# Half steps of the output product in front of the fourth attention, earlier table loads, filter norms on channel columns, and a third slot for half modulation units

## The reference, cut to what matters

```
mod = silu(c) @ ada_w + ada_b                  # six modulation rows of 2048
h = rmsnorm(x) * (1 + sc1) + sh1
o_a, o_b, o_c, o_d = four attention mixers(h @ w_in)   # 8 heads of 64 each
#   o_d = gate0 * compressed(15 blocks) + gate1 * selected + gate2 * window
x = x + g1 * (concat(rmsnorm(o_m) for m) @ w_out)
x = x + g2 * mixture_of_16_experts(...)
# second block
h = sin-MLP(positions) @ w4 * decay            # filters, forward and backward
k = [h_fwd, 0, h_bwd[:0:-1]];  k = k / sum(|k|, over positions)
k_f = rfft(k);  y = long convolution with k_f, spatial gating, output product
x = x + swiglu(...)
```

## Time and profile before

| | |
|---|---|
| median of 3 runs | 2988.32 us (2987.99 to 2994.21) |
| profiled execution | 2990.0 us |
| its span, first to last instruction | 2987.8 us |
| mean granted TensorE clock | 0.953 |
| TensorE / VectorE / ScalarE busy | 91% / 63% / 43% |
| data moved | 651.10 MB |

### The profile page before, as it was taken

One profiled execution on the slowest core, in us unless ns is written; L12 is line 12 of the kernel. 1 busy time (PEld: TensorE's weight loads), 2 busy tenths in 40 slices (PEclk: granted clock), 3 DMA queues, 4 the chain that ended last, 5 costly groups with the idle time before them and its releaser, 6 DMA issues.

```text
span 2987.8 us, 36422 instructions
## 1 busy us (share of the span) xinstructions
PE 2721.8 (91%) x14284; PEld 2275.7 (76%) x14284; DVE 1880.4 (63%) x2425; ACT 1276.5 (43%) x1540; POOL 28.9 (1%) x50
## 2 busy tenths in 40 slices
PE   3769998897999999999698898999899999999997
PEld 1258887676788787777498396999778888888886
DVE  6987755576666888888766544454555544445444
ACT  2024543442444577777433043533344444443443
POOL 1000000000000000000000000000000000000000
PEclk9789998797999999999899997999999999999999
DMA  9787675351777899999354152554455555555553
GB/s 347 302 331 268 247 290 182 118 196 42 253 249 264 277 332 372 372 360 368 145 183 178 61 204 86 182 183 170 154 183 174 192 193 189 193 187 196 187 194 113
DMA packets 181342, 651.10 MB, mean 218 GB/s; under 512 B 12363, under 2 KB 12428, under 8 KB 136920
## 3 DMA queue, kind: packets, MB, share of 16 engines
q1 hardware_dynamic: 170208, 593.53, 55.9%
q0 software_dynamic: 8160, 37.17, 3.3%
q10 hardware_dynamic: 2840, 18.56, 1.7%
HBM read 641.82 MB, written 13.68 MB: 219 GB/s over the span
## 4 chain that ended last, share of the span: by engine, by line
PE 69%; DVE 14%; DMA 8%; ACT 5%; issue 3%; DVEq 0%; ACTq 0%; SPq 0%
PE ps L1586 68%; DMA raw<-in_stream 6%; DVE w_lo L923 3%; DVE raw L1002 2%; ACT w_hi L588 2%; DMA under_r<-in_stream 1%; DVE under_r L1020 1%; ACT arena L703 1%; ACT arena L609 1%; DVE arena L984 1%; DVE arena L1082 0%; DVE ps L1136 0%; PE ps L1685 0%; DVE arena L1098 0%; DVE h_lo L974 0%
## 5 line engine op out<-in xcount | busy, mean ns | idle before, releaser
L923 DVE TENSOR_TENSOR w_lo<-raw,w_hi 128x1024 fp32r<-128x1024 f32 x968 | 1170.2, 1223 | 800.4 <-ACT w_hi L588 797.4
L588 ACT ACTIVATE w_hi<-raw 128x1024 fp32r<-128x1024 f32 x968 | 1010.8, 1057 | 940.4 <-PE ps L1586 845.8
L1586 PE MATMUL ps<-w_hi,h_hi 128*128 128x512 f32 x1216 | 476.8, 392 | 15.9 <-DVE h_lo L1545 10.0
L1586 PE MATMUL ps<-w_hi,r_hi 128*128 128x512 f32 x1184 | 469.6, 397 | 14.2 <-DVE w_lo L923 7.1
L1586 PE MATMUL ps<-w_lo,h_hi 128*128 128x512 f32 x1216 | 475.1, 391 | 0.0
L1586 PE MATMUL ps<-w_hi,h_lo 128*128 128x512 f32 x1216 | 475.1, 391 | 0.0
L1586 PE MATMUL ps<-w_lo,r_hi 128*128 128x512 f32 x1184 | 462.6, 391 | 0.0
L1586 PE MATMUL ps<-w_hi,r_lo 128*128 128x512 f32 x1184 | 462.5, 391 | 0.0
L1586 PE MATMUL ps<-h_hi,w_hi 128*128 128x256 f32 x1536 | 443.6, 289 | 17.0 <-DVE w_lo L923 8.5
L1586 PE MATMUL ps<-h_lo,w_hi 128*128 128x256 f32 x1536 | 440.1, 287 | 0.0
L1586 PE MATMUL ps<-h_hi,w_lo 128*128 128x256 f32 x1536 | 439.8, 286 | 0.0
(11 more groups left out here) (268 smaller groups left out, 1839.9 us busy)
## 6 DMA issues: line engine op xcount, KB each, us to landing
raw<-in_stream SPq DMA_DIRECT2D x524, 1024.0 KB, 5.5
under_r<-in_stream SPq DMA_DIRECT2D x80, 512.0 KB, 5.3
arena<-in_mod_units ACTq DMA_DIRECT2D x16, 1024.0 KB, 4.9
bias_skew<-bias_rows POOLq DMA_DIRECT2D x4, 1536.0 KB, 21.4
filters<-arena POOLq DMA_DIRECT2D x4, 1280.0 KB, 5.1
arena<-filters POOLq DMA_DIRECT2D x4, 1280.0 KB, 6.0
x<-in_x POOLq DMA_DIRECT2D x1, 2048.0 KB, 19.7
arena<-bias_skew POOLq DMA_DIRECT2D x2, 1024.0 KB, 7.5
```

What stands on the lines that cost most here:

```text
L588: act.activation(dst, src, ACT.Copy).then_inc(hi_ready, 1)
L923: dve.tensor_tensor(low, src, high, ALU.subtract).then_inc(lo_ready, 1)
L1586: return pe.matmul(o, a, b, start=start, stop=stop)
```

## The change

1. *Filter norms on channel columns.* TensorE multiplies the absolute taps (as weights) with one column of ones, which gives the sums as 128x4; VectorE takes the reciprocal of that. ScalarE makes four diagonal matrices of it, TensorE spreads them with the matrix of ones, and ScalarE copies the result to `rnorm`. The row's `memset` goes: its taps come from a copy of the hidden layer whose first column is zero.
2. *A third slot.* Half units aside have three places, and each is loaded when the third last is summed up. The third place lies in part where the filters were, so SyncE waits for the last filter store.
3. *Table loads.* `spread_rows(1)`, three of the four compression loads and `spread_rows(3)` are issued during and after the first attention and in the second.
4. *The gap.* Half steps 0 to 7 of the output product, the splits of half steps 3 to 10, six half units aside and the first `part_out` stand between the parts of the compression. The fourth attention has one half step a turn and half units in ten turns. The compression's scores and transposes use banks 2 and 3.
5. `nsa_out` multiplies both gates in one instruction.

```diff
-FOURTH_HALVES = 16
+FOURTH_HALVES, GAP_HALVES, GAP_ASIDES = 16, 8, 6
...
+        rn_cols, rn_diag = stat[:, 156:160], at(13856, 4, P)
...
-            half = slice(j % 2 * HALF, (j % 2 + 1) * HALF)
+            half, last = slice(j % 2 * HALF, (j % 2 + 1) * HALF), under_r[:, 1, D + HALF:2 * D]
             if j < ASIDE_HALVES - FOURTH_HALVES:
-                return under_r[:, 1, D + j % 2 * HALF:D + (j % 2 + 1) * HALF], c_row[:, half]
-            return under_r[:, j % 2, D + HALF:2 * D], c_fourth[:, half]
+                return (under_r[:, 1, D:D + HALF], last, at(11936, HALF))[j % 3], c_row[:, half]
+            return (under_h[:, 0, 0:HALF], last, under_h[:, 0, HALF:D])[j % 3], c_fourth[:, half]
...
-            return range(3 * t // 2, 3 * (t + 1) // 2) if t < 16 else range(0)
+            return range(GAP_HALVES + t, GAP_HALVES + t + 1) if t < 16 else range(0)
...
-                if j >= 2:
-                    sp.wait_ge(sem("aside_done"), j - 1)
+                if j >= 3:
+                    sp.wait_ge(sem("aside_done"), j - 2)
                 if j == ASIDE_HALVES - FOURTH_HALVES:
-                    sp.wait_ge(sem("c_moved"), 1)
+                    sp.wait_ge(half_done, 8 * gp)
...
             weight(4)
+            sp.wait_ge(sem("kf_stored1"), 32)
+            aside(2)
...
+            for k in range(5):
+                part_weight(k)
+            aside(used + 3)
+            aside(used + 4)
+            aside(used + 5)
+            part_weight(6)
+            aside(used + 6)
+            aside(used + 7)
+            aside(used + 8)
+            used += GAP_ASIDES
...
+            pool.wait_ge(sem("att_out"), 2)
+            spread_rows(1)
+            pool.wait_ge(sem("att_out"), 16)
+            load("ld_cmp", (w1v, d["w1v"]), (w2c, d["w2kv"]), (peT, d["pe"]))
+            pool.wait_ge(sem("att_out"), 18)
+            spread_rows(3)
             pool.wait_ge(sem("att_out"), 16 * 2)
-            spread_rows(1)
             toeplitz(1, toep2)
-            load("ld_cmp", (w1k, d["w1k"]), (w1v, d["w1v"]), (w2c, d["w2kv"]), (peT, d["pe"]))
-            spread_rows(3)
+            load("ld_cmp", (w1k, d["w1k"]))
...
+            act.wait_ge(sem("sin_out"), 3)
+            act.activation(at(F_R, 1, parts=64), at(F_H, 1, parts=64), ACT.Copy, scale=0.0).then_inc(sem("sin_out"), 1)
+            act.activation(at(F_R + 1, P - 1, parts=64), at(F_H + 1, P - 1, parts=64), ACT.Copy).then_inc(sem("sin_out"), 1)
...
+                act.wait_ge(sem("rn_ready"), b + 1)
+                for q in range(4):
+                    ins = act.activation(rn_diag[:, q, :], ident, ACT.Copy, scale=rn_cols[:, q:q + 1])
+                ins.then_inc(sem("rn_act"), 1)
+                if b >= 2:
+                    act.wait_ge(sem("spectrum_out"), 5 * (b - 1))
+                act.wait_ge(sem("rn_spread"), b + 1)
+                copy(rnorm[b % 2], ps[:, 2, :]).then_inc(sem("rn_act"), 1)
...
             exps(16, 8, True, "d_q", qT2)
+            hi(gp, 3)
             norm_root("mixB", ("att_out", 48), 512, mix, mix_junk)
+            hi(gp, 4)
...
+            hi(gp, 5)
             act.wait_ge(sem("c_moved"), 1)
             norm_hi("mixB", r_hi, 4, mixf, 8)
+            hi(gp, 6)
+            hi(gp, 7)
             for r in range(4):
...
+                if r == 1:
+                    part_out(0)
+                if r < 3:
+                    hi(gp, 8 + r)
...
-                    if n == 1:
-                        ch(ins)
-                        ins = dve.memset(taps[b % 2][0:1, 1, :], 0.0)
...
-                ch(dve.reciprocal(rnorm[b % 2], ps[:, 2, :]))
+                if b:
+                    dve.wait_ge(sem("rn_act"), 2 * b)
+                dve.reciprocal(rn_cols, ps[:, 2, 0:4]).then_inc(sem("rn_ready"), 1)
...
             scores(16, 8, True, head_out, toep2, "d_q")
+            lo(gp, 3)
             mixer_unit("mixB", 48)
+            lo(gp, 4)
...
-            mixer_split(1, "mixB", 2)
+            lo(gp, 5)
             dve.wait_ge(sem("cmp_exp"), 1)
             dve.tensor_tensor(v15(cp), v15(cp), keep, ALU.mult).then_inc(sem("cmp_p"), 1)
+            mixer_split(1, "mixB", 2)
+            lo(gp, 6)
...
+            lo(gp, 7)
+            first_fourth = ASIDE_HALVES - FOURTH_HALVES
+            aside_half(first_fourth)
+            aside_half(first_fourth + 1)
+            lo(gp, 8)
+            aside_half(first_fourth + 2)
+            lo(gp, 9)
...
+                if q == 0:
+                    aside_half(first_fourth + 3)
+                    lo(gp, 10)
+                    aside_half(first_fourth + 4)
+                    aside_half(first_fourth + 5)
...
-                for half in range(TH):
-                    ch(dve.tensor_tensor(rden[:, half:half + 1], rden[:, half:half + 1],
-                                         gates[:, half, 3 * h + branch:3 * h + branch + 1], ALU.mult))
+                ch(dve.tensor_tensor(rden, rden, gates[:, :, 3 * h + branch], ALU.mult))
...
+                pe.wait_ge(sem("abs_ready"), 4 * b + 4)
+                if b:
+                    pe.wait_ge(sem("rn_act"), 2 * b)
+                for q in range(4):
+                    for n in range(4):
+                        ins = mm(ps[:, 2, q:q + 1], taps_abs[b % 2][:, n, q * P:(q + 1) * P], ones[:, 0:1], n == 0, n == 3)
                 ins.then_inc(sem("norm_mm"), 1)
+
+            def norm_spread(b):
+
+                pe.wait_ge(sem("rn_act"), 2 * b + 1)
+                for q in range(4):
+                    ins = mm(ps[:, 2, q * P:(q + 1) * P], ones[:, :], rn_diag[:, q, :])
+                ins.then_inc(sem("rn_spread"), 1)
...
             ins.then_inc(sem("cmp_s"), 1)
+            part(0)
+            part(1)
             turn("mixB", 4, mix)
+            part(2)
+            part(3)
             pe.wait_ge(sem("cmp_p"), 1)
             for r in range(4):
...
                 ins.then_inc(sem("cmp_t"), 1)
+                part(4 + r)
                 pe.wait_ge(sem("cmp_pt"), r + 1)
...
-            pe.wait_ge(sem("att_out"), 50)
```

More of the change, by code:

```diff
@@ L464, in _, with part_weight @@
                 for _ in range(ASIDE[k]):
-                    aside(used + 2)
+                    aside(used + 3)
                     used += 1
+            def part_weight(k):
+                if k % 2 == 0 and len(ASIDE) // 2 + k // 2 + 5 < BASE["moe"]:
+                    weight(len(ASIDE) // 2 + k // 2 + 5)
+            for k in range(5):
+                part_weight(k)
+            aside(used + 3)
+            aside(used + 4)
[5 more added lines that the diff above has]
+            used += GAP_ASIDES
             for t in range(16):
                 for k in share(t):
[L469 to L472, removed]
+                    part_weight(k)
+                if t < FOURTH_HALVES - GAP_ASIDES:
+                    aside(used + 3)
                     used += 1
@@ L682, in values_out, with part_out @@
                 return step
+            def part_out(cb):
+                act.wait_ge(half_done, 8 * gp + 6 * cb + 6)
+                copy(abc_sum[:, :, 512 * cb:512 * cb + 512], ps[:, 6:8, :]).then_inc(sem("part_out"), 1)
             def exps(first, n, sink, beside=None, dst=None, partial=False):
@@ L689, in exps @@
                 for t in range(n + 1):
-                    if partial and t and t % 4 == 0:
-                        cb = t // 4 - 1
-                        act.wait_ge(half_done, 8 * gp + 6 * cb + 6)
-                        copy(abc_sum[:, :, 512 * cb:512 * cb + 512], ps[:, 6:8, :]).then_inc(sem("part_out"), 1)
+                    if partial and t % 6 == 4:
+                        part_out(t // 6 + 1)
                     if t < n:
@@ L1651, in make_taps @@
                         pe.wait_ge(sem("taps_ready"), 4 * b + n - 1)
-                    mm(ps[:, n % 2, :], arena[0:64, F_H + (n // 2) * P:F_H + (n // 2 + 1) * P],
+                    rows_of = F_R if n == 1 else F_H + (n // 2) * P
+                    if 4 * b + n == 1:
+                        pe.wait_ge(sem("sin_out"), 5)
+                    mm(ps[:, n % 2, :], arena[0:64, rows_of:rows_of + P],
                        w4[:, b, (n % 2) * 512:(n % 2 + 1) * 512]).then_inc(sem("taps_mm"), 1)
             def taps_norm(b):
-                for n in range(4):
-                    pe.wait_ge(sem("abs_ready"), 4 * b + n + 1)
-                    ins = mm(ps[:, 2, :], ones[:, :], taps_abs[b % 2][:, n, :], n == 0, n == 3)
-                ins.then_inc(sem("norm_mm"), 1)
+                pe.wait_ge(sem("abs_ready"), 4 * b + 4)
[4 more added lines that the diff above has]
+                        ins = mm(ps[:, 2, q:q + 1], taps_abs[b % 2][:, n, q * P:(q + 1) * P], ones[:, 0:1], n == 0, n == 3)
+                ins.then_inc(sem("norm_mm"), 1)
+            def norm_spread(b):
[3 more added lines that the diff above has]
+                ins.then_inc(sem("rn_spread"), 1)
             make_taps(0)
@@ L1724, in attend @@
```

(18 more changed lines are left out.)

24 lines of the change are left out of this document (14 added, 10 removed).

## The result

The changed kernel takes 2969.8 us (median of four runs, 2965.1 to 2973.9) against 2989.7 for the kernel before (four runs, 2988.0 to 2994.2; the table ahead of the prediction has three of them): a ratio of 0.9926, 95% interval 0.9913 to 0.9939. Measured once more beside its variants it gives 2973.4 against 2989.8, ratio 0.9939 (0.9927 to 0.9951). So it is faster by 0.6 to 0.7%, 16 to 20 us. The forecast was 2967 with a range of 2955 to 2982. The profiled execution took 2971.0 (span 2968.9), 19 less than the one of before; its sum was forecast at 2968.2.

The account below looks back on a forecast made before the run. VectorE was taken to bound the prologue, and a VectorE-ScalarE chain the fourth attention, despite TensorE's 91%. Gains 13.3 + 6.4 + 2.1 = 21.8 us off 2990.0 give 2968.2; with the median 1.7 lower, forecast 2967, range 2955 to 2982.

Parts of the forecast that it names:

- What bounds: Whole kernel: TensorE works 91% of the span, but VectorE sets the pace in the first 180 us.
- the transfers set the pace: Rival, chance 0.18: the stream fails at 332 GB/s or half units land as late as now; 2977 us.
- Norms: Prologue: smaller reciprocals and no memsets on VectorE save 13.3 us, bounds 5 and 16.
- The reciprocal wait: Prologue sign: VectorE's wait for the norm sum near 5 us in the first block, none later.
- Third slot and tables: 404 to 485 us: TensorE's waits for half units and following half clock go; 6.4 us gained, bounds 0 and 9.
- The two waits of TensorE: 404 to 485 us: TensorE's waits for low parts, 4.4 us, taken as gone.
- The gap: Before the fourth attention: work moved in makes its first scores reach VectorE 12.3 us later.
- a gap at half clock: Rival, chance 0.13: the stretch before the fourth attention stays at half clock, costing 15.6 us; 2983 us.
- the filling does not fill: Rival, chance 0.05: half steps queue serially at half clock before the fourth attention, adding 41 us there; 2995 us.
- The fourth attention: Fourth attention: one half step a turn, not bound by TensorE; 15 us less, with 0.6 of tail taken off.
- the ring: Fourth attention: VectorE's scores, ScalarE's exponentials, copy and split, VectorE's low part set the turn; 5.73 us with one half step.
- The multiply: Attention outputs: one fewer multiply each, hidden while VectorE waits for ScalarE; priced at nothing, 2.6 us without that cover.

Follow-up runs that it names:

- old_norms: Changed kernel with the filter norms taken back to the 128x512 reciprocal and the zero-row memset; 2984.8 us, ratio 0.9976 to the kernel before.
- norm_twice: Changed kernel with every column of the filter norms computed twice, 32 instead of 16 one-column products a block; 2986.6 us, ratio 0.9982 to the kernel before.
- slots_tables: Changed kernel with two places for half units and GpSimd's table loads in the old order; 2982.8 us, ratio 0.9968 to the kernel before.
- two_slots: Changed kernel with two places for half units instead of three, table loads in their new place; 2977.8 us, ratio 0.9946 to the kernel before.
- hi_first4: Changed kernel with ScalarE's copy for a later split at the head of the turn, fourth attention only; 2965.1 us, ratio 0.9911 to the kernel before.
- hi_all_gap_undone: Changed kernel with ScalarE's copy at the turn's head in all four attentions, and half steps, splits and half units back in the fourth; 2945.9 us, ratio 0.9843.
- gap_undone: Changed kernel with half steps, splits and half units back in the fourth attention, third slot kept; 2976.8 us, ratio 0.9949 to the kernel before.

## Why the prediction was right, point by point

**What bounds.** Right for the prologue: VectorE is busy 29.4 of 30 us with the same stream, and what is taken from it comes off the end (old_norms, norm_twice). The rival that the transfers set the pace has fallen: the stream kept up at 339 GB/s, above the 332 it was said to need, and no wait for it appeared inside the modulation runs.

**Norms, 13.3 forecast.** 11.0 us between the first splits, 11.5 counted from the chunk with the DMA wait, 10.7 in the experiment. The first block gave 1.2 and not 1.8: from that chunk (49.03 before) to the end of the division it took 18.4 us before and 17.2 after. The price of a column in the first block was right (6.98 us for 32 instructions, 0.218 each, the upper bound), and so was its reason, the slow pace of this stretch: in the second block the same 32 take 3.63 us, 0.113 each, below the lower bound of 0.13. But the columns start at 59.48 and not at 58.4; 0.44 of that is a later start of the stream, the other 0.6 is the first block's shortfall, and VectorE waits 0.47 in it for a tap product. The reciprocal wait was forecast "near 5" and is 3.12. That figure did not follow from the prediction's own sum, which has the columns end at 65.4 and VectorE ready at 62.3 (64.05 less its wait of 1.06 and the memset's 0.65), a wait of 3.1. The later blocks gave 3 x 3.85 less 1.27: VectorE now waits 0.54, 0.27 and 0.46 us for TensorE's tap products, which the memset and the long reciprocal used to cover. That cover is the part that the sum missed.

**Third slot and tables, 6.4 forecast.** The ledger shows 3.7 to the compression, and slots_tables 5.7 in the same stretch; both lie within the bounds of 0 and 9. The waits lay behind the second attention, and that part alone shows more: from its last score to the compression's first product it takes 71.4 us before, 65.9 in the changed kernel, 66.0 and 66.1 with one measure undone and 71.0 with both. That is 5.2 to 5.5 of the 6.4 (other runs with the same three slots and tables took 63.5 to 66.4 in this part, so its size is known to some 2 us). The rest of the ledger's gap is 2.7 us lost ahead of it, between the first and the second attention (52.65 before, 55.37 now), and the repeat of the same program does not lose them (52.65 again): scatter. The two waits of TensorE (4.4 us) are gone and the 5.14 us at the compression are there, as said. What was missed is where the slot pays: either measure alone clears this stretch, and the third slot's own worth is in the gap. The prediction added up its parts as if they were independent.

**The gap, 12.3 forecast.** 12.3 measured, and the steps hold: the wait in front of half step 4 is 1.79 (forecast 1.4), the clock is at its lower level until after the scores, 0.74 in the next 7.2 us (1.9 us lost, forecast 2.1), 1.00 to 542.2, and 0.91 in the last 19.7, which costs 1.8 us (forecast 1.5 "for clock lost after such a wait"). The rival of a gap at half clock has fallen, and so has the one in which the filling does not fill. It held only because six half units could land in time; with two slots this part takes 47.0 us (two_slots) and 45.2 (slots_tables), not 42.65.

**The fourth attention, 15 less 0.6 forecast.** 17.05 measured. The turns are the forecast ones: seven of 5.73, two of 6.23 with a modulation sum, a first one of 5.36, and six of 4.58, the last one behind the last score. By the prediction's own span, from the first score to the division behind the last turn, it is 101.65 before and 85.40 now (561.86 to 647.26): 16.25 less, where 85.7 + 1.0 was forecast. The 1.0 for TensorE's own turn at the end did not come in this execution; in the repeat the last turns take 4.7 to 4.8. The other 0.8 us came behind it, where the eight transposes for mixer D's norm took 1.97 us before and 1.09 now; the prediction had put 0.6 us on the wrong side there. That the ring and not TensorE sets these turns, its main claim, is shown by hi_first4 for the attention of now. For the one of before it holds by a narrow margin: its pair of turns took 12.6 us on VectorE where TensorE, busy for 98.54 of 98.60 us, made its scores 7.47 and 4.75 us apart, 12.2 a pair, and ran ahead. The same layout with the ring shortened takes 90.2 us from first to last score (hi_all_gap_undone) against 94.4 (gap_undone), so "not bound by TensorE" was worth 4.2 us there, against 11.35 in the attention of now.

**The multiply, 0 forecast.** 0 in the turns.

**The sum.** 11.0 + 3.7 + 4.8 = 19.5 against 21.8, with 0.6 lost behind. Three terms were each off by two to three us, and the errors partly cancel. One of the three is scatter (the 2.7 us behind the first attention); the cover of the norms and the attention's gain were mis-sized. So the forecast was right within 3 us with some luck: the mechanisms held, and their sizes did less well than the whole shows.

## What to carry to other kernels

An engine that looks busy in a stage may still be waiting inside a ring of others: compare the turn with the engine's own work in it (4.75 us for TensorE against turns of 5.73 here), then ask which member of the ring does work in it that nobody in this turn needs. Putting that work in front of the wait instead of behind it was worth 38 us, twice the whole change, for four lines moved. Where the engine has enough work of its own, as TensorE in the fourth attention of before, the same ring costs little. Parts of a change that supply and use the same buffers are not to be added: price the consumer with and without the supply, and each cure for a stall with the other one in place.

## What the runs showed of the hardware that was not expected

**The clock falls in different places in executions of one kernel.** Behind the first attention TensorE stands still for a while; windows of 6 us, first in the profiled execution of the changed kernel, then in its repeat, which is 1.7 us later in its work:

```profile
290.00:296.00 6.00, 3.80 (x27) 3.33 (x25) 4.20 (x12) 3.25 (x9) 0.00 (x0) 0.87 0.70 254
296.00:302.00 6.00, 6.00 (x32) 6.00 (x32) 3.08 (x13) 3.00 (x7) 1.62 (x3) 0.56 0.51 162
```

```profile
290.00:296.00 6.00, 4.82 (x40) 4.55 (x40) 3.73 (x11) 2.71 (x8) 0.00 (x0) 1.00 0.46 165
296.00:302.00 6.00, 5.56 (x47) 5.42 (x47) 3.88 (x11) 2.87 (x8) 1.09 (x3) 1.00 0.55 199
```

In the first the granted clock falls, to a mean of 0.56 in the second window; in the repeat it stays at 1.00. TensorE issues 32 instructions in one and 47 in the other. From the first split to the compression's first product this makes 276.6 and 274.9 us for one program; old_norms, which differs only ahead of that stretch, takes 272.0, and two_slots 277.5. A term of 2 to 4 us read from one pair of traces over that stretch is within this scatter, and a gain in the prologue can be given back there: 11.0 us at the first split were 9.1 at the start of the second attention.

**The clock row does not tell the pace of the first 75 us.** The changed kernel's profile shows a granted clock of 1.00 both while the 32 column products take 6.98 us (59.48) and while they take 3.63 (84.31). Products of one form with 512 columns show the same step in between: four take 3.20 us at 73.52 (0.8 each), six take 2.74 at 77.44 (0.46 each), also at 1.00. There the durations of a known product tell the pace, and the row does not; why the row shows 1.00 stays open.
